# Attention heads of a hybrid decoder step: a second buffer for copied scores, convolution taps spread round the chain, and one channel block's taps in PSUM among the projections

## The reference, cut to what matters

```python
proj = h @ w_in
u = glu_a * jax.nn.sigmoid(glu_g)
c, conv_new = causal_dwconv(u, conv_prev, conv_w, conv_b)     # 31 taps, 512 channels
...
z = jnp.einsum('bqhd,bkhd->bhqk', q, k) * (SB_HEAD_DIM ** -0.5) + bias
lb = jnp.where(mask, jax.nn.log_sigmoid(-z), 0.0)
rev = lax.cumsum(lb, axis=3, reverse=True)
after = jnp.concatenate([rev[..., 1:], jnp.zeros_like(rev[..., :1])], axis=-1)
wgt = jnp.where(mask, jnp.exp(jax.nn.log_sigmoid(z) + after), 0.0)
o = jnp.einsum('bqhk,bkhd->bqhd', wgt, v)
...
mixed = jnp.concatenate([a_out, o], axis=-1)                   # a_out = silu(layernorm(c))
return mixed @ w_out, conv_new, k, v
```

## Time and profile before

| | us |
|---|---|
| median of three runs | 2514.54 |
| lowest and highest of them | 2511.38, 2514.76 |
| the profiled execution's own time | 2511.32 |
| its span, first to last instruction | 2509.6 |

### The profile page before, as it was taken

The page is one execution under the profiler, slowest core; times in us unless marked ns, Lnnn a source line. Parts: engine busy times, 40 slices in busy tenths (PEclk is TensorE's granted clock), DMA queues, the critical chain, the costliest instruction groups (busy, mean ns, idle before and its releaser), DMA issues. The chain is left out here.

```text
span 2509.6 us, 44037 instructions
## 1 busy us (share of the span) xinstructions
PE 2353.5 (94%) x18361; PEld 2241.0 (89%) x18361; DVE 1339.4 (53%) x1540; ACT 798.6 (32%) x984; POOL 410.6 (16%) x296
## 2 busy tenths in 40 slices
PE   7999999987779999999999999898989879999997
PEld 7999999873359999999999998888888868999997
DVE  4443445778855443445443444767676757553453
ACT  4222222223332221223221223453535343222223
POOL 0000012680002000003000003010101015455440
PEclk8999999987789999999999999899999999999999
DMA  4323326572523323323323323313232312546542
GB/s 138 84 83 102 91 73 187 148 205 78 151 76 82 86 83 101 85 74 109 100 72 107 90 75 98 85 52 89 68 89 68 93 55 65 156 119 184 135 130 95
DMA packets 430918, 254.88 MB, mean 102 GB/s; under 512 B 12162, under 2 KB 407786, under 8 KB 430752
## 3 DMA queue, kind: packets, MB, share of 16 engines
q1 hardware_dynamic: 430295, 253.08, 36.0%
q10 hardware_dynamic: 508, 0.18, 0.0%
HBM read 239.30 MB, written 14.60 MB: 101 GB/s over the span
## 5 line engine op out<-in xcount | busy, mean ns | idle before, releaser
L220 PE MATMUL PS<-hh,wh 128*128 128x260 f32 x3792 | 776.6, 286 | 25.1 <-DVEq L645 7.6
L220 PE MATMUL PS<-hh,wl 128*128 128x260 f32 x3792 | 768.9, 285 | 0.0
L220 PE MATMUL PS<-hl,wh 128*128 128x260 f32 x3792 | 768.6, 285 | 0.0
L220 PEld LDWEIGHTS PS<-hh,wh 128*128 128x128 f32 x3792 | 590.2, 190 | 38.5 <-issue 23.7
L220 PEld LDWEIGHTS PS<-hh,wl 128*128 128x128 f32 x3792 | 589.1, 190 | 0.3
L220 PEld LDWEIGHTS PS<-hl,wh 128*128 128x128 f32 x3792 | 588.9, 190 | 0.4
L197 DVE TENSOR_TENSOR wl<-raw,wh 128x2048 fp32r<-128x2048 f32 (+2 forms) x194 | 453.7, 2339 | 207.5 <-ACT wh L193 206.7
L193 ACT ACTIVATE wh<-raw 128x2048 fp32r<-128x2048 f32 (+2 forms) x194 | 352.7, 1818 | 317.4 <-PE PS L220 281.7
L220 PE MATMUL PS<-hid_l,wh 128*128 128x260 f32 x1408 | 283.7, 283 | 0.0
L220 PE MATMUL PS<-hid_h,wh 128*128 128x260 f32 x1408 | 283.3, 282 | 0.0
L220 PE MATMUL PS<-hid_h,wl 128*128 128x260 f32 x1408 | 283.0, 282 | 0.0
(11 more groups left out here) (303 smaller groups left out, 2376.8 us busy)
## 6 DMA issues: line engine op xcount, KB each, us to landing
raw<-in_ffn_gate_dram SPq DMA_DIRECT2D x88, 512.0 KB, 4.0
raw<-in_ffn_up_dram SPq DMA_DIRECT2D x88, 512.0 KB, 5.2
raw<-in_ffn_down_dram SPq DMA_DIRECT2D x64, 384.0 KB, 3.9
raw<-in_ffn_down_dram SPq DMA_DIRECT2D x64, 320.0 KB, 3.6
raw<-in_m_in_proj_dram SPq DMA_DIRECT2D x40, 512.0 KB, 5.2
ms_b<-in_state_ssm_dram SPq DMA_DIRECT2D x64, 256.0 KB, 5.0
page<-in_cache_sb_v_dram SPq DMA_DIRECT2D x48, 256.0 KB, 2.9
raw<-in_ab_in_proj_dram SPq DMA_DIRECT2D x20, 512.0 KB, 5.3
```

The costliest lines, as they stand in the source:

```text
L220: ins = pe.matmul(out, x[:, k0, c:c + m], y[:, k, half * H2:(half + 1) * H2], start=k == 0 and a == 0, stop=k == nk - 1 and a == 2)
```

## The change

It does five things.

1. The copy of the scores moves in front of the exponential in `front`, and goes into two buffers in turn, `zc` and the weight buffer `raw[:, 1]`. It waits for t of two heads back in place of t of the head before.
2. So that `raw[:, 1]` is free, the split of output-projection slot 1 moves from iteration 4 to iteration 0, on ScalarE and VectorE; the second copy waits for it. The load of slot 3, which lands in the same buffer, moves behind the last t.
3. VectorE's order in an iteration becomes 6 taps, max and mask of head i, 3 taps, t of head i - 1, 3 taps, and the weight mask.
4. The 31 taps of channel block 0 move into the projections: one behind each of reduces 3, 4, 5, 6, 8 and 9, from step 3 on, until 31 are done (the place of number 9 is passed in every step, though most have no reduce there).
5. Block 0 accumulates in PSUM bank 4, and its last tap writes `cbuf`. TensorE waits for that tap before the transposes of v in step 9, which use bank 4.

```diff
@@ -753,6 +753,7 @@
                 ktok, tl, krow, vrow = page[:, 0:NTT, :], page[0:PADW + B, NTT, :], page[0:B, NTT + 1, :], qrow[:, :]
+                zcopy = [zc[:, :], raw_view(1, 1, W).rearrange("p a c -> p (a c)")]
                 cst = zc[:, 0:2 * HD].rearrange("p (a c) -> p a c", a=2)
@@ -767,7 +768,7 @@
                 names = ("conv_in small_in masks tr_done cp_done u_done u0_mm u0_free u1_free gate_sig d_chain "
-                         "ln_cc ln_sq ln_ms ln_var ln_sd ln_cn ln_act ln_hi conv_done "
+                         "ln_cc ln_sq ln_ms ln_var ln_sd ln_cn ln_act ln_hi conv0_done conv_done "
                          "qrow_tr qrow_cp qb_mm qb_cp key_in0 key_in1 v_tr v_cp misc_tr misc_cp row_cp kv_out "
@@ -856,10 +857,9 @@
                         load_page("cache_sb_v", (g * VQ + j) * NPG + pg, vplace[i % NV], val_in[i % NV])
-                        if i == vstart(5) + NV:
-                            load_static(sp, N0 + KS + 3)
-
-                    for n in range(KS + 4, NS_A + 2):
+
+                    sp.wait_ge(S["t_done"], NH)
+                    for n in range(KS + 3, NS_A + 2):
                         load_static(sp, N0 + n)
@@ -941,6 +941,7 @@
                         if i == 9:
+                            pe.wait_ge(S["conv0_done"], 1)
                             v_tokens(0)
@@ -1147,14 +1148,16 @@
                             .then_inc(S["abs_done"], 1)
+                        if h >= 2:
+                            act.wait_ge(S["t_done"], h - 1)
+                        if h == 1:
+                            act.wait_ge(w_ready, N0 + KS + 4)
+                        act.activation(zcopy[h % 2], z_ps, ACT.Identity, scale=SCALE, bias=biasb[:, h:h + 1])\
+                            .then_inc(S["z_cp"], 1)
                         act.wait_ge(S["abs_done"], h + 1)
                         act.activation(s, s, ACT.Ln, bias=1.0).then_inc(S["lnp_done"], 1)
-                        if h >= 1:
-                            act.wait_ge(S["t_done"], h)
-                        act.activation(zc[:, :], z_ps, ACT.Identity, scale=SCALE, bias=biasb[:, h:h + 1])\
-                            .then_inc(S["z_cp"], 1)

@@ -1163,6 +1166,7 @@
                             front(i)
+                            hi_static(act, N0 + KS + 1)
                         if i <= 1:
@@ -1187,8 +1191,6 @@
                                 .then_inc(S["pv_hi"], 1)
-                        if i == 4:
-                            hi_static(act, N0 + KS + 1)
                         for g in range(B // VQ):
@@ -1221,13 +1223,17 @@
                     def conv_step(c, w):
-                        out, col = cbuf[:, c, 0:T], cwv[:, w * CB + c:w * CB + c + 1]
+                        col = cwv[:, w * CB + c:w * CB + c + 1]
+                        acc = PS[:, 4, :] if c == 0 else cbuf[:, c, 0:T]
                         if w == 0:
-                            ch(dve.tensor_scalar(out, uA[:, c, w:w + T], col, vec[:, V_CB + c:V_CB + c + 1],
+                            ch(dve.tensor_scalar(acc, uA[:, c, w:w + T], col, vec[:, V_CB + c:V_CB + c + 1],
                                                  ALU.mult, ALU.add))
                         else:
-                            ch(dve.scalar_tensor_tensor(out=out, in0=uA[:, c, w:w + T], scalar=col, in1=out,
+                            out = cbuf[:, 0, 0:T] if c == 0 and w == CW - 1 else acc
+                            ch(dve.scalar_tensor_tensor(out=out, in0=uA[:, c, w:w + T], scalar=col, in1=acc,
                                                         op0=ALU.mult, op1=ALU.add))
+                        if c == 0 and w == CW - 1:
+                            dve.sem_inc(S["conv0_done"], 1)

@@ -1237,6 +1243,7 @@
                     pos = [0]
+                    EARLY = (3, 4, 5, 6, 8, 9)

@@ -1301,6 +1308,8 @@
                                 reduce(sum(REDUCES[:i - ES]) + r)
+                            if i > QS and r in EARLY:
+                                conv(min(1, CW - pos[0]))
                             if r == 2:
@@ -1322,20 +1331,24 @@
                             dve.wait_ge(S["dscore"], 1)
-                        conv(16)
-                        if 1 <= i <= NH:
-                            dve.wait_ge(S["sum_mm"], i)
-                            dve.tensor_tensor(sp_[:, (i - 1) % NSP, :], zc[:, :],
-                                              PS[:, 3:6, :].rearrange("p b c -> p (b c)")[:, 0:W],
-                                              ALU.subtract).then_inc(S["t_done"], 1)
+                        conv(6)
                         if i < NH:
                             dve.wait_ge(S["z_cp"], i + 1)
-                            dve.scalar_tensor_tensor(out=s, in0=zc[:, :], scalar=0.0, in1=s, op0=ALU.max, op1=ALU.add)\
-                                .then_inc(S["sp_max"], 1)
+                            dve.scalar_tensor_tensor(out=s, in0=zcopy[i % 2], scalar=0.0, in1=s, op0=ALU.max,
+                                                     op1=ALU.add).then_inc(S["sp_max"], 1)
                             dve.wait_ge(S["sp_max"], i + 1)
                             diagonal(s).then_inc(S["sp_done"], 1)
+                        if i == 0:
+                            lo_static(dve, N0 + KS + 1)
+                        conv(3)
+                        if 1 <= i <= NH:
+                            dve.wait_ge(S["sum_mm"], i)
+                            dve.tensor_tensor(sp_[:, (i - 1) % NSP, :], zcopy[(i - 1) % 2],
+                                              PS[:, 3:6, :].rearrange("p b c -> p (b c)")[:, 0:W],
+                                              ALU.subtract).then_inc(S["t_done"], 1)
+                        conv(3)
                         if i == 1:
@@ -1363,8 +1376,6 @@
                                 .then_inc(S["pv_lo"], 1)
-                        if i == 4:
-                            lo_static(dve, N0 + KS + 1)
                         if i == NH - 1:
```

## The result

The changed kernel takes 2490.11 us (median of four runs, 2488.09 to 2490.97) against 2512.96 for the kernel before (2510.55 to 2514.76): a ratio of 0.9911, 95% interval 0.9899 to 0.9923, some 23 us less. The forecast was 2498 (2487 to 2510).

What follows compares the result with a forecast made beforehand. VectorE and the ring through ScalarE and TensorE were taken to pace the heads; heads -25.8, clock +4.5 and projections +6.6 sum to -14.7 us, 2496.6 from 2511.32; starting from 2513 instead, the forecast was 2498 (2487 to 2510).

Steps and rivals of the forecast that it cites:

- Sum: Whole kernel: heads -25.8, clock +4.5 and projections +6.6 us give -14.7 us against the profiled execution before.
- the ring: Heads: chain of t, scores' copy, scores, product and sums across engines, pacing them with VectorE at 18.4 us an iteration before.
- Projections: Steps 3 to 8 of the projections: block 0's taps in PSUM, 785 ns each, lengthen them by +6.6 us in all.
- Part (a): Heads, first max to iteration 3: fewer taps and waits, against the moved split and a logarithm wait; -4.8 us.
- Part (b): Heads, iteration 3 to the t of iteration 7: 76 taps become 57 and copy waits go; -18.8 us.
- share of the clock: Heads: TensorE's product at the low clock level in two products of five; +4.5 us, ends 0 and +14.8.
- Part (c): Last iteration of the heads: copy, max and one mask leave the path from t to the next product; -2.3 us.
- Edits at nothing: Slot 3's load behind the last t, and ScalarE's waits before its score copies: no cost expected.
- A tap in one bank: Rival, projections: a tap reading and writing one PSUM bank takes 1.25 us, total 2512 us; chance 0.07.
- Taps amid GpSimd: Rival, projections: taps collide with GpSimd's products and take 1.74 us each, total 2527 us; chance 0.06.
- TensorE wasn't low all through: Rival, heads: TensorE sets the pace at 1.2 GHz, the low clock, total 2508.6 us; chance 0.13.

Runs made afterwards that it cites:

- e4_no_taps_heads: Changed kernel with 90 of the 93 taps of the heads left out (blocks 1 to 3 keep only their first tap): 2482.82 us.
- e3_taps_in_sbuf: Changed kernel with block 0 accumulated in SBUF instead of PSUM bank 4: 2507.00 us.
- e9_combined: Changed kernel in VectorE's old order, with taps shifted to where VectorE idled and the pair's split ahead of t: 2477.49 us.
- e7_buffers_alone: Changed kernel with VectorE's old order (12 taps, t, then max and masks), keeping two buffers and early taps: 2485.48 us.
- e7_again: The kernel of e7_buffers_alone measured once more: 2483.52 us.
- e8_buffers_only: Kernel before with two buffers, early copy and moved weight split; old order, sixteen taps, none in the projections: 2496.31 us.

## Why the prediction was right, and which terms were off

Sum: -14.7 forecast, -20.4 in the profiled executions. The time, 2490.11, lies near the fast end of the range.

- **What bounds the heads.** VectorE with the ring was right, but the new pace was not VectorE's 14.2 us: iterations take 13.4 to 17.3 (15.5 on average, 14 to 16 were expected), with VectorE idle for 22 of the 108.6 us, and e4_no_taps_heads shows 13.9 without its taps.
- **Projections**, +6.6: measured +5.5. The tap came as the nearest row had it (748 ns); the gate products, 1.3 us shorter in all, I hadn't counted.
- **Part (a)**, first max to iteration 3, -4.8: measured 43.4 against 48.2, -4.8. Head 1's logarithm ends 16.2 us after the first max, where I had 16.5, and VectorE waits 2.46 for it. The order's price was in this number, unnamed: with the old order the first t comes 5.7 us sooner.
- **Part (b)** with its share of the clock, -18.8 + 4.5 = -14.3: measured 72.7 against 86.2, -13.6. Two products of five ran low, as guessed, and t waited 3.01 and 2.55 for them where I had 2. That count was luck: I guessed it from the gap in front, and the trace of before has a product behind 0.65 us of idle time that took 4.03, where the earlier trace rows has 2.37 behind the same gap:

```profile
653.12 4.03 PE L1022 MATMUL PS<-spl,vtok 128*64 128x512 f32 x8 [0.65 <-DVE spl L1282]
```

- **Part (c)**, -2.3: measured 13.38 against 18.54, -5.2. This is the mis-sized term: the path from t to the product is 2.34 shorter (4.33 for 6.67), as counted, but I left the product as it was. Before it ran low, and after it runs high (2.34); that is 2.2 more, and the value pages behind it give 0.7. The windows give that iteration a clock of 0.82 and 1.00. The product before:

```profile
708.73 4.50 PE L1022 MATMUL PS<-spl,vtok 128*64 128x512 f32 x8 [4.56 <-DVE hl L1363]
```

- Not in the sum: the first max comes 0.6 us sooner after the scaling, the stretch behind the last t is 0.5 shorter, and 1.4 lie outside the mixer's stretch.
- **Edits at nothing** cost nothing that shows: the load of slot 3 now starts at 703.8, and the first to last addition of the output projection takes 37.5 us in both traces.
- **The rivals.** A tap in one bank took 748 ns, not 1,250. Taps amid GpSimd didn't collide, and e3_taps_in_sbuf shows that they would have in SBUF, by 0.4 us each, so that rival's mechanism was real and the choice of PSUM was what kept it away. TensorE wasn't low all through.

What I didn't weigh is whether the parts pull the same way. They don't: buffers -16, taps -13, order +6, by the times.

## What to carry to other kernels

When a change has several parts, cost the new order by itself. Here placing the taps where VectorE idled, the first iterations above all, won as much as the whole old order did; that an operation whose inputs are ready should not stand behind one that waits for a later result fits e9_combined, but no run parts it cleanly from the places of the taps. A second buffer for a copied tile paid where the timeline showed a producer held for its release, and work moved from a full stage to one with slack paid more with its accumulator where another engine's reads don't meet it. After each such step look again at which chain sets the pace: here the ring through TensorE, ScalarE and VectorE's own t and mask, 13 to 15 us, took over from the taps.

## What the runs showed of the hardware

- The level of TensorE's clock is not told by the gap just ahead. In the timeline after, a product behind 2.27 us of idle time takes 4.50 and one behind 2.74 takes 2.34. In e9_combined one behind 2.10 takes 3.99, between the two levels' times:

```profile
635.75 2.37 PE L1023 MATMUL PS<-spl,vtok 128*64 128x512 f32 x8
...
649.24 3.99 PE L1023 MATMUL PS<-spl,vtok 128*64 128x512 f32 x8 [2.10 <-DVE spl L1291]
```

- Amid GpSimd's products the gate product, with two SBUF inputs, takes 1.69 to 1.71 us without taps in the projections, 1.27 to 1.30 with taps in PSUM, and 1.57 to 1.62 in e3_taps_in_sbuf, against 0.70 alone. The timelines show what goes with it: when it starts, GpSimd's running product, by GpSimd's spans, which are rough, has 1.15 us left in the kernel before (479.12 to 480.27), 0.72 after (481.25 to 481.97) and 1.05 in e3_taps_in_sbuf (484.76 to 485.81), and the gate product is longer than 0.70 by 1.01, 0.57 and 0.90. No run moves that overlap by itself.
- What lies outside the mixer's stretch, which no edit here touches directly, differs by 8 us between profiled executions (2204.6 to 2212.5 in the traces of before, after, e7_buffers_alone, e7_again, e8_buffers_only and e9_combined), so one trace's total tells differences below that badly. The mixer's stretch repeats better: 283.4 and 284.1 in two traces of the changed kernel, 273.5 and 273.4 in two of the old order.
